# Odd mixer's attention: order of the three PE groups of a step, a later weighing, a third buffer

## The reference, cut to what matters

```python
def gqa_block_attention(q, k, v):
    ...
        s = jnp.einsum('bqgrd,bkgd->bgrqk', q_blk, k).astype(jnp.float32) * scale
        p = jax.nn.softmax(s, axis=-1).astype(v.dtype)
        return jnp.einsum('bgrqk,bkgd->bqgrd', p, v)
...
def odd_mixer(x, mix_norm, w_qkv, q_norm, k_norm, w_out):
    proj = rms_norm_2(x, mix_norm) @ w_qkv
    ...
    return gqa_block_attention(q, k, v) @ w_out
```

## Time and profile before

| | |
|---|---|
| median of 3 runs | 2733.45 us (2733.14 to 2735.53) |
| the profiled execution | 2732.53 us |
| its span on the core | 2730.7 us |
| mean granted clock of PE | 0.995 |
| busy share of the span | PE 97%, PEld 77%, DVE 54%, ACT 38%, POOL 29% |

### The profile page before, as it was taken

One profiled execution on the slowest core, in us unless ns is written; L12 is line 12 of the kernel. 1 busy time (PEld: TensorE's weight loads), 2 busy tenths in 40 slices (PEclk: granted clock), 3 DMA queues, 4 the chain that ended last, 5 costly groups with the idle time before them and its releaser, 6 DMA issues. The chain is left out here.

```text
span 2730.7 us, 40699 instructions
## 1 busy us (share of the span) xinstructions
PE 2651.9 (97%) x15358; PEld 2095.1 (77%) x15358; DVE 1477.6 (54%) x1873; ACT 1041.7 (38%) x1858; POOL 793.5 (29%) x740
## 2 busy tenths in 40 slices
PE   8999999899999999999999998999999999999998
PEld 6888888656787788888777765888887656888887
DVE  4477673374654777754577666544434366634432
ACT  6433332334355333332346455322222367322221
POOL 3231111351666421122004564311112064311100
PEclk9999999999999999999999999999999999999999
DMA  4233323311200233333221121332333200223233
GB/s 157 77 93 100 93 90 97 107 62 48 68 12 23 82 96 97 95 91 102 80 78 54 43 71 35 100 100 92 98 91 104 85 16 2 91 94 100 90 92 103
DMA packets 80552, 219.16 MB, mean 80 GB/s; under 512 B 21917, under 2 KB 22045, under 8 KB 80158
## 3 DMA queue, kind: packets, MB, share of 16 engines
q1 hardware_dynamic: 79262, 215.17, 25.7%
q10 hardware_dynamic: 1152, 2.10, 0.2%
HBM read 215.14 MB, written 2.10 MB: 80 GB/s over the span
## 5 line engine op out<-in xcount | busy, mean ns | idle before, releaser
L334 PE MATMUL psum<-rounded,high_r 128*128 128x512 f32 x3024 | 1192.5, 394 | 29.6 <-DVE rounded L422 9.9
L336 PE MATMUL psum<-rounded,high_r 128*128 128x512 f32 x3024 | 1179.9, 390 | 0.0
L338 PE MATMUL psum<-rounded,ring_low 128*128 128x512 f32 x3024 | 1179.9, 390 | 0.0
L359 ACT ACTIVATE high_r<-ring 128x1024 fp32r<-128x1024 f32 (+2 forms) x432 | 420.3, 973 | 1373.7 <-PE psum L338 1345.9
L364 DVE TENSOR_TENSOR ring_low<-ring,high_r 128x1024 fp32r<-128x1024 f32 (+2 forms) x430 | 522.2, 1214 | 541.0 <-ACT high_r L359 539.3
L334 PEld LDWEIGHTS psum<-rounded,high_r 128*128 128x128 f32 x3024 | 569.1, 188 | 181.3 <-issue 35.2
L338 PEld LDWEIGHTS psum<-rounded,ring_low 128*128 128x128 f32 x3024 | 569.4, 188 | 119.8
L336 PEld LDWEIGHTS psum<-rounded,high_r 128*128 128x128 f32 x3024 | 569.9, 188 | 117.3 <-issue 1.4
L808 DVE TENSOR_TENSOR arena<-psum,inverse 128x512 f32<-128x512 f32 x176 | 121.5, 691 | 314.4 <-PE psum L338 314.2
L661 POOL CAST rounded<-rows 128x512 f32 (+1 forms) x88 | 53.8, 611 | 785.7 <-DVE rows L813 785.7
L457 POOL TENSOR_TENSOR arena<-resid 128x512 f32<-128x512 f32 x41 | 53.2, 1298 | 234.6 <-DVE resid L445 234.6
(11 more groups left out here) (425 smaller groups left out, 2754.3 us busy)
## 6 DMA issues: line engine op xcount, KB each, us to landing
ring<-in_up SPq DMA_DIRECT2D x176, 512.0 KB, 3.5
ring<-in_down SPq DMA_DIRECT2D x64, 384.0 KB, 3.1
ring<-in_down SPq DMA_DIRECT2D x64, 320.0 KB, 2.9
ring<-in_even_in SPq DMA_DIRECT2D x36, 512.0 KB, 3.5
ring<-in_sgu_in SPq DMA_DIRECT2D x16, 512.0 KB, 3.5
ring<-in_even_out SPq DMA_DIRECT2D x16, 384.0 KB, 3.1
ring<-in_qkv SPq DMA_DIRECT2D x12, 512.0 KB, 3.5
ring<-in_sgu_out SPq DMA_DIRECT2D x8, 512.0 KB, 3.5
```

The source lines that it names most:

```text
L334: nc.tensor.matmul(psum[:, m, :], high_r[:, r % HIGHS, blk], x_high, start=(k0 + k == 0), stop=False)
L336: nc.tensor.matmul(psum[:, m, :], high_r[:, r % HIGHS, blk], x_low, start=False, stop=False)
L338: mm = nc.tensor.matmul(psum[:, m, :], ring_low[:, r % R, blk], x_high, start=False, stop=end)
L359: nc.scalar.activation(high_r[:, r % HIGHS, 0:nk * P], ring[:, r % R, 0:nk * P], ACT.Copy).then_inc(unit_high, 1)
```

## The change

PE's step is cut into three functions, `score` (S), `turn` (T) and `weigh` (W), and their order depends on the step: an odd step i is S(i), T(i - 3), W(i - 5); an even step is W(i - 5), T(i - 3), S(i). Weighing is five steps behind the scores (it was four), so there is one more step at the end. `spread` and `rotate` stay last in their steps. The buffers `pt` are three, the third in two tiles of the arena at 26, and the copies wait for the weighing three back in place of two. The orders of ACT, DVE and POOL stay as they are.

```diff
--- before.py
+++ after.py
@@ -3206,7 +3206,7 @@
             scale_of = HD ** -0.5
             vt = span(VT, 2).rearrange("p (c f) -> p c f", c=NCH)
             pr = [arena[:, 32 + 2 * i:34 + 2 * i, :] for i in range(4)]
-            pt = [arena[:, 40 + 2 * i:42 + 2 * i, :] for i in range(2)]
+            pt = [arena[:, at:at + 2, :] for at in (40, 42, 26)]
             mx, nm, sm, rc = (small[:, 16 * a:16 * a + 16] for a in range(4))
             cosine = [arena[:, 24 + i, :] for i in range(2)]
             sine = [rows[:, 2 + i, :] for i in range(2)]
@@ -3309,55 +3309,66 @@
                             for s in range(3 * (n - 9) // 2, 3 * (n - 9) // 2 + 3):
                                 rotate(s)
 
+                    def score(i):
+                        j, qt = divmod(i, 4)
+                        if qt == 0:
+                            pe.wait_ge(roped, 3 + j)
+                        if i == 0:
+                            pe.wait_ge(scaled, scaled_before + TILES)
+                        if i >= 2:
+                            pe.wait_ge(expd, 2 * (i - 1))
+                        for e in range(2):
+                            mm = nc.tensor.matmul(psum[:, i % 2 * 2 + e, :], arena[half(e), Q + j, qt * P:(qt + 1) * P],
+                                                  arena[half(e), K + j // 4, :], start=True, stop=True)
+                        mm.then_inc(scored, 1)
+
+                    def turn(u):
+                        pe.wait_ge(first_normed, u + 1)
+                        pe.wait_ge(second_normed, u + 1)
+                        if u:
+                            pe.wait_ge(first_turned_kept, u)
+                            pe.wait_ge(second_turned_kept, u)
+                        else:
+                            pe.wait_ge(v_kept, 2)
+                        for e in range(2):
+                            for b in range(4):
+                                tr = nc.tensor.transpose(psum[:, 4 + e, b * P:(b + 1) * P],
+                                                         pr[u % 4][:, e, b * P:(b + 1) * P], con("ident"))
+                        tr.then_inc(turned, 1)
+
+                    def weigh(u):
+                        j, qt = divmod(u, 4)
+                        pe.wait_ge(first_turned_kept, u + 1)
+                        pe.wait_ge(second_turned_kept, u + 1)
+                        if qt == 0 and j:
+                            pe.wait_ge(out_low, j)
+                        for b in range(4):
+                            for e in range(2):
+                                mm = nc.tensor.matmul(psum[half(e), 6, qt * P:(qt + 1) * P], vt[:, b, value_cols(j, e)],
+                                                      pt[u % 3][:, e, b * P:(b + 1) * P], start=(b == 0), stop=(b == 3))
+                        mm.then_inc(pv_done, 1)
+
                     def step(i):
-                        if i < STEPS:
-                            j, qt = divmod(i, 4)
-                            if qt == 0:
-                                pe.wait_ge(roped, 3 + j)
-                            if i == 0:
-                                pe.wait_ge(scaled, scaled_before + TILES)
-                            if i >= 2:
-                                pe.wait_ge(expd, 2 * (i - 1))
-                            for e in range(2):
-                                mm = nc.tensor.matmul(psum[:, i % 2 * 2 + e, :], arena[half(e), Q + j, qt * P:(qt + 1) * P],
-                                                      arena[half(e), K + j // 4, :], start=True, stop=True)
-                            mm.then_inc(scored, 1)
+                        if i % 2 and i < STEPS:
+                            score(i)
                         if i == 1:
                             turn_values(0)
                             turn_values(1)
+                        if i % 2 == 0 and i >= 5:
+                            weigh(i - 5)
                         if 3 <= i < STEPS + 3:
-                            u = i - 3
-                            pe.wait_ge(first_normed, u + 1)
-                            pe.wait_ge(second_normed, u + 1)
-                            if u:
-                                pe.wait_ge(first_turned_kept, u)
-                                pe.wait_ge(second_turned_kept, u)
-                            else:
-                                pe.wait_ge(v_kept, 2)
-                            for e in range(2):
-                                for b in range(4):
-                                    tr = nc.tensor.transpose(psum[:, 4 + e, b * P:(b + 1) * P],
-                                                             pr[u % 4][:, e, b * P:(b + 1) * P], con("ident"))
-                            tr.then_inc(turned, 1)
-                        if i >= 4:
-                            u = i - 4
-                            j, qt = divmod(u, 4)
-                            pe.wait_ge(first_turned_kept, u + 1)
-                            pe.wait_ge(second_turned_kept, u + 1)
-                            if qt == 0 and j:
-                                pe.wait_ge(out_low, j)
-                            for b in range(4):
-                                for e in range(2):
-                                    mm = nc.tensor.matmul(psum[half(e), 6, qt * P:(qt + 1) * P], vt[:, b, value_cols(j, e)],
-                                                          pt[u % 2][:, e, b * P:(b + 1) * P], start=(b == 0), stop=(b == 3))
-                            mm.then_inc(pv_done, 1)
+                            turn(i - 3)
+                        if i % 2 == 0 and i < STEPS:
+                            score(i)
+                        if i % 2 and i >= 5:
+                            weigh(i - 5)
                         if 1 <= i <= 8:
                             if i % 2:
                                 spread(FIRST + i // 2)
                             else:
                                 rotate(FIRST + i // 2 - 1)
                     products(pe, name, two_parts(XH, XL), scaled, after_unit=beside, bank_of=bank_of)
-                    for i in range(STEPS + 4):
+                    for i in range(STEPS + 5):
                         step(i)
 
                 @block.scalar
@@ -3404,9 +3415,9 @@
                         if 3 <= i < STEPS + 3:
                             u = i - 3
                             act.wait_ge(turned, u + 1)
-                            if u >= 2:
-                                act.wait_ge(pv_done, u - 1)
-                            nc.scalar.activation(pt[u % 2][:, 0, :], psum[:, 4, :], ACT.Copy).then_inc(first_turned_kept, 1)
+                            if u >= 3:
+                                act.wait_ge(pv_done, u - 2)
+                            nc.scalar.activation(pt[u % 3][:, 0, :], psum[:, 4, :], ACT.Copy).then_inc(first_turned_kept, 1)
                         if i < STEPS:
                             act.wait_ge(negated, i + 1)
                             if i >= 4:
@@ -3490,9 +3501,9 @@
                         if 3 <= i < STEPS + 3:
                             u = i - 3
                             dve.wait_ge(turned, u + 1)
-                            if u >= 2:
-                                dve.wait_ge(pv_done, u - 1)
-                            nc.vector.tensor_copy(pt[u % 2][:, 1, :], psum[:, 5, :]).then_inc(second_turned_kept, 1)
+                            if u >= 3:
+                                dve.wait_ge(pv_done, u - 2)
+                            nc.vector.tensor_copy(pt[u % 3][:, 1, :], psum[:, 5, :]).then_inc(second_turned_kept, 1)
                         if 1 <= i <= 8:
                             if i % 2:
                                 head_scale(FIRST + i // 2)
```

## The result

Over 22 runs each, the kernel before has a median of 2735.44 us and the changed kernel of 2746.47. The ratio is 1.0038, with a 95% interval of 1.0031 to 1.0044: +10.4 us (8.5 to 12.0), where +9.9 was forecast.

What follows compares the result with a forecast made beforehand. PE, busy in 97% of the span, was taken to bound the kernel. Ten pairs +8.0, up to S(10) +2.0 and the tail -0.1 give +9.9 us on 2733.45: 2743.3 us, range 2738.5 to 2750.

Steps and rivals of the forecast that it cites:

- The joins: Attention, PE: neighbouring S save 0.21 us, neighbouring W 0.09; a pair without waits takes 5.92 us, not 6.22.
- T before S: PE's even step: the one new turn, taken as 1.02 us; at 1.06, +0.5 us for all pairs.
- The read-out: Bank 6, read by ACT and DVE: W's waits for it go, 0.44 us a pair.
- The wait of T: T(o-3) behind two S waits for DVE's copy, starting 3.45 us after S(o-1); PE idles 1.54 us a pair.
- Nothing else is later in the pair: S(10) to S(30): T(o-2), S(o+2) and the third buffer add no wait; a pair takes 7.46 us.
- The sum: Whole kernel: +8.0 + 2.0 - 0.1 = +9.9 us, giving 2743.3 us.
- The ten pairs: S(10) to S(30): 74.6 us in place of 66.63, +8.0 us.
- Up to S(10): Attention's first steps: late T, +0.27 us for o = 5, 7, 9, and T(7) ahead of S(10); +2.0 us together.
- The tail: After S(30) to odd_out: 15.2 us in place of 15.26, -0.1 us; bounds -1.8 to +0.6.
- The faster one: Attention: turns saved, read-out hidden and T doesn't wait; -8.3 us, 2725 us; chance 0.07.
- Same, with a shorter wait: Ten pairs: T's wait at most 1.1 us each, time within 5.5 us of before; chance 0.10.
- The clock: PE's granted clock falls after waits, some 1.3 us a fall; 2747 to 2757 us; chance 0.10.

Runs made afterwards that it cites:

- both orders: Changed kernel with DVE's and ACT's step orders rearranged, both copies ahead of what they waited behind; ratio 0.9977 to the kernel before.
- the other bank: Changed kernel, but from T(7) on DVE's half of T goes by turns to PSUM banks 7 and 5; ratio 1.0000 to the kernel before.
- the copy first: Changed kernel, but in even steps DVE does copy(i-3) ahead of max(i); ratio 1.0025 to the kernel before.
- the longer chain: Changed kernel with one more DVE reduction, about 0.7 us, ahead of the maximum in even steps 10 to 30; ratio 1.0092 to the kernel before.
- the missing reversal: Later weighing and third buffer alone, every step S(i), T(i-3), W(i-5), none reversed; ratio 1.0068 to the kernel before.

## Why the prediction was right, point by point

*The joins.* Right in sign; the two W were mis-sized. Two S take 1.91 to 1.92 us to the T that follows, read where that T doesn't wait, in the experiments with both orders and with the other bank (1.91 from the earlier trace rows). Two W take 1.89 (2249.52 to 2251.41) and not 1.97: the row I took ends in the turn to `odd_out`'s first matmul. T before S, of which no row was shown, takes 1.03 where I took 1.02. The Trainium skill (TensorEngine Tiling (Array Packing), section Tiling Modes, Key Properties) says that a change of the tiling mode drains the engine; the two joins, 0.20 and 0.17 us cheaper than two groups apart, agree.

*The read-out.* Right: no W waits for it any more.

*The wait of T.* Right to 0.01 us: 3.45 from S(o-1) to T's weights. The experiments with the bank and with the copy first show both halves of the reason, the shared bank and DVE's order; the longer chain shows that this ring sets the period.

*Nothing else is later in the pair.* Right for a pair of 7.4 us; that ACT's copy would be the next to hold T shows only in a shorter one.

*The sum.* The ten pairs: +7.68 where +8.0 stood. Nine take 7.39 or 7.40 us where 7.46 was worked out, most of it the W join; one takes 7.76, because DVE stood for 0.30 us ahead of a reciprocal with nothing waited for. Up to S(10): +1.70 where +2.0 stood; a T behind a rotate starts 3.41 us after S(o-1) and not 3.45, so 0.23 late and not 0.27, and here too the W join saves more than 0.09. The tail: -0.22 where -0.1 stood. Together the stage gives +9.16 where +9.9 was worked out. That the runs' +10.4 is still nearer is in part luck: their interval is 3.5 us wide.

*The rivals.* The faster one failed where it was said to: DVE gets to the copy after the maximum; moving it, and ACT's with it, gave that rival its sign. "Same, with a shorter wait" did not come. The clock stayed at 1.00 from S(10) to `odd_out` in the profiled execution, with waits of 1.49 us, one of 1.68 and one of 1.85; in the longer chain it fell behind seven of ten waits of 2.2 and more.

What stays open: the runs' ratio, +10.4 us (8.5 to 12.0), holds the stage's 9.16 and doesn't need more. The granted clock over whole executions speaks against further falls: the changed kernel's 22 runs lie between 0.990 and 0.996 with a median of 0.993, the runs of the kernel before, listed beside the experiments, between 0.989 and 0.995 with medians of 0.993 and 0.992, and the longer chain's four between 0.988 and 0.990. A fall in single executions can't be excluded.

## What to carry to other kernels

When groups of one engine are joined to save the turns between them, look for the buffer that the next group needs back, and count from the group that starts the other engine's chain to the group that needs its end: here S, maximum, copy, T was 3.45 us, and the change cut PE's work in between from a T, a W and an S to a single S. Here the orders of the engines that serve the joined groups had to change with them; when they did, the same order of PE was 6.3 us faster than before and not 10.4 slower. And ask for the second-longest ring before moving the first: with one wait taken away, the next, of 0.5 us, came to light.

## What the runs showed of the hardware

A wait of PE can cost more than its length. In one order of PE's groups, waits of 1.49 us in each pair, and one of 1.85, left the granted clock at 1.00. Waits of 2.22, and one of 2.57, at the same place were followed by a fall in seven of ten pairs; they brought the mean to 0.87 and cost 11.3 us beside the 7.3 of the longer waits themselves, while one product of 1.06 us in each wait brought back 1.00. The prediction's price of some 1.3 us a fall was near the 1.6 estimated here; what it had open was which waits bring one.

The length alone doesn't decide. The wait of 1.41 to 1.42 us ahead of S(2) stands in all nine profiled executions, behind the same groups of PE. In six of them the groups behind it took longer (S(2) or the rotate 2.08 us and not 1.13 or 1.12), as in the earlier trace rows; in three, those of the copy first, the longer chain and the missing reversal, they took 1.13 and 1.12, and the clock was 1.00 from S(0) to S(10). Why the same wait brings a fall in one execution and none in another, no run here shows.
